# Around the turn between head pairs: where a gate store, a norm read and a staging copy are waited for

## The reference, cut to what matters

```python
h = _rmsnorm(x, W['g_pre_mix'][l])
proj = h @ W['w_in'][l]
qa, fa, ia, ga, qb, kb, vb, uc, gl = jnp.split(proj, _split_points(), axis=-1)
# A) HGRN2: chunkwise gated recurrence, then
oa = _rmsnorm(oa.astype(dt), W['a_norm'][l]) * jax.nn.silu(ga.reshape(Bn, T, A_HEADS, A_DV))
# B) stick-breaking attention over qb, kb, vb; for the samples with K/V from the paged cache
# C) u = ua * sigmoid(ug), causal depthwise conv w=31, LayerNorm, silu
m = gates[:, :, 0] * ya + gates[:, :, 1] * yb + gates[:, :, 2] * yc
out = m @ W['w_o'][l]
```

## Time and profile before

| | us |
|---|---|
| median of 3 runs | 2222.81 (2222.72 to 2224.42) |
| profiled execution, its own time | 2222.81 |
| its span | 2221.0 |
| PE busy in the span | 2048.0 (92%) |
| DVE busy | 1085.8 (49%) |
| ACT busy | 606.7 (27%) |
| POOL busy | 574.7 (26%) |
| DMA, mean rate | 71 GB/s |

### The profile page before, as it was taken

The page is one execution under the profiler, slowest core; times in us unless marked ns, Lnnn a source line. Parts: engine busy times, 40 slices in busy tenths (PEclk is TensorE's granted clock), DMA queues, the critical chain, the costliest instruction groups (busy, mean ns, idle before and its releaser), DMA issues.

```text
span 2221.0 us, 32175 instructions
## 1 busy us (share of the span) xinstructions
PE 2048.0 (92%) x12832; PEld 1957.6 (88%) x12832; DVE 1085.8 (49%) x1169; ACT 606.7 (27%) x792; POOL 574.7 (26%) x392
## 2 busy tenths in 40 slices
PE   6899998999899998999788897799999999999993
PEld 5899997999799997999678897599999999999993
DVE  4187646886387645786247523622221322222136
ACT  3235422462335522562234212310010100101011
POOL 1211211221111211221123323423233332332322
PEclk9999999999899999999899998899999999999997
DMA  4121213111221213112443412111111011111131
GB/s 148 49 88 49 73 45 102 55 60 53 69 89 49 71 39 109 50 61 68 157 150 116 120 60 104 74 33 48 47 38 57 28 52 42 42 54 31 57 111 78
DMA packets 203987, 156.89 MB, mean 71 GB/s; under 512 B 15730, under 2 KB 188402, under 8 KB 203890
## 3 DMA queue, kind: packets, MB, share of 16 engines
q1 hardware_dynamic: 201698, 146.89, 21.3%
q10 hardware_dynamic: 2192, 8.65, 1.0%
HBM read 120.16 MB, written 35.35 MB: 70 GB/s over the span
## 4 chain that ended last, share of the span: by engine, by line
PE 85%; DVE 7%; ACT 4%; DMA 2%; issue 1%; POOL 0%; SPq 0%; POOLq 0%; ACTq 0%; DVEq 0%
PE psum L370 73%; PE psum L674 3%; PE psum L629 2%; PE psum L607 2%; PE psum L618 1%; PE psum L575 1%; DVE hid L1529 1%; PE psum L656 1%; DVE mix L1514 1%; PE psum L638 1%; DMA g_d<-gate_logits 1%; DVE x_again L1508 1%; DVE arena L1206 1%; DMA gates<-g_d 0%; DVE hid_lo L1531 0%
## 5 line engine op out<-in xcount | busy, mean ns | idle before, releaser
L370 PE MATMUL psum<-h_hi,w_hi 128*128 128x352 f32 x2400 | 541.7, 334 | 37.1 <-DVE h_lo L1210 9.9
L370 PE MATMUL psum<-h_lo,w_hi 128*128 128x352 f32 x2400 | 522.0, 326 | 0.0
L370 PE MATMUL psum<-h_hi,w_lo 128*128 128x352 f32 x2400 | 522.0, 325 | 0.0
L370 PEld LDWEIGHTS psum<-h_hi,w_hi 128*128 128x128 f32 x2400 | 407.9, 192 | 63.1 <-issue 41.9
L370 PEld LDWEIGHTS psum<-h_hi,w_lo 128*128 128x128 f32 x2400 | 415.7, 190 | 0.0
L370 PEld LDWEIGHTS psum<-h_lo,w_hi 128*128 128x128 f32 x2400 | 413.6, 191 | 0.0
L360 POOL CAST w_hi<-w_raw 128x512 fp32r<-128x512 f32 (+1 forms) x128 | 97.9, 765 | 733.9 <-PE psum L370 642.7
L347 POOL CAST w_hi<-w_raw 128x1024 fp32r<-128x1024 f32 x60 | 64.1, 1068 | 827.0 <-PE psum L370 807.7
L362 POOL TENSOR_TENSOR w_lo<-w_raw,w_hi 128x512 fp32r<-128x512 f32 (+1 forms) x128 | 227.0, 1773 | 10.3
L1176 ACT ACTIVATE hid<-psum 128x1056 f32<-128x1056 f32 x32 | 33.7, 1054 | 583.1 <-PE psum L370 583.1
L1538 DVE TENSOR_TENSOR ff_sum<-ff_sum,psum 128x1056 f32<-128x1056 f32 x56 | 70.2, 1254 | 227.5 <-PE psum L370 227.5
(11 more groups left out here) (237 smaller groups left out, 2382.3 us busy)
## 6 DMA issues: line engine op xcount, KB each, us to landing
w_raw<-in_w_in SPq DMA_DIRECT2D x60, 512.0 KB, 4.0
w_raw<-in_w_ff SPq DMA_DIRECT2D x32, 512.0 KB, 4.0
w_raw<-in_w_ff SPq DMA_DIRECT2D x64, 256.0 KB, 2.7
g_d<-gate_logits SPq DMA_DIRECT2D x24, 528.0 KB, 2.8
gates<-g_d SPq DMA_DIRECT2D x24, 528.0 KB, 3.7
arena<-in_xT SPq DMA_DIRECT2D x8, 528.0 KB, 7.4
x_again<-in_xT SPq DMA_DIRECT2D x1, 4224.0 KB, 15.2
x_d<-x_again ACTq DMA_DIRECT2D x8, 528.0 KB, 2.7
```

The costliest lines, as they stand in the source:

```text
L370: mm = pe.matmul(ps[:, b0 + g, 0:GW], w[:, slot, k, :], x[:, k, g * GW:(g + 1) * GW], start=(k == 0 and w is wh and x is xh), stop=(k == k ...
```

## The change

Five edits, in the fences below; nothing is computed differently.

1. **Gate stores.** ACT's wait for both gate-store semaphores at the group's end goes. `stage_unit` waits at every gate unit for the last store of its own buffer. The semaphores start at one (`before` = 1, a DVE memset adds it), so that the first group has nothing to wait for.
2. **Norm sums.** H_FILL (4, 4, 4) becomes (4, 4, 2, 2): two of the last four pieces of unit 13 now stand behind the norm sums. ACT copies unit 13 after the two activations of the norm.
3. **The wait for the norm read** moves from the end of PE's group to the start of the next one.
4. **Scores.** In step q = 0 `scores(p, 1, 0)` stands behind the first three pieces, no longer ahead of them.
5. **Turned inputs.** ACT copies unit 8 (and waits for `kv_stored`) after the first level exponential, no longer ahead of the copy of the turned inputs.

```diff
-H_FILL = (4, 4, 4)
+H_FILL = (4, 4, 2, 2)
...
-        n_done, n_read, rs_ready = S("oa_norm_sum", 1), S("oa_norm_read", 1), S("oa_rstd", 1)
+        n_done, n_read, rs_ready = S("oa_norm_sum", 1), S("oa_norm_read", 1, 1), S("oa_rstd", 1)
...
-        gl_stored = [S("gate_stored0", 16 * ((GPG + 1) // 2)), S("gate_stored1", 16 * (GPG // 2))]
+        gl_stored = [S("gate_stored0", 16 * ((GPG + 1) // 2), 1), S("gate_stored1", 16 * (GPG // 2), 1)]
...
                 staged.wait(pe, p, -2)
+                n_read.wait(pe, p, 0)
                 scores(p, 0, 0)
...
-                    if q + 1 < QB:
+                    if q and q + 1 < QB:
                         scores(p, q + 1, 0)
                     fill(A_FILL[0])
+                    if q == 0:
+                        scores(p, 1, 0)
...
                 mm.then_inc(n_done.sem, 1)
-                n_read.wait(pe, p, 1)
+                fill(H_FILL[3])
...
                 if g is not None:
-                    if g >= 2:
-                        gl_stored[g % 2].wait(act, p, 16 * (g // 2))
+                    gl_stored[g % 2].wait(act, p, 16 * (g // 2))
...
                 read_values(QB - 1)
-                if more:
-                    kv_stored.wait(act, p, 32)
-                stage_unit(8, p, more)
                 ia_turned.wait(act, p, 1)
...
                     act.activation(A(B_W[j % 2], n), A(B_D, n), ACT.Exp).then_inc(wexp.sem, 1)
+                    if j == 0:
+                        if more:
+                            kv_stored.wait(act, p, 32)
+                        stage_unit(8, p, more)
...
-                stage_unit(13, p, more)
                 n_done.wait(act, p, 1)
...
                 act.activation(A(B_RS, T), A(B_RS, T), ACT.Exp, scale=-0.5).then_inc(rs_ready.sem, 1)
+                stage_unit(13, p, more)
                 if more:
                     oa_ready.wait(act, p, 1)
                     h_stored.wait(act, p, 32)
-                    for b in range(2):
-                        gl_stored[b].wait(act, p, 16 * ((GPG - b + 1) // 2))
...
+            dve.memset(cwp[:, 1:2], 0.0).then_inc(n_read.sem, 1)
+            dve.memset(cwp[:, 2:3], 0.0).then_inc(gl_stored[0].sem, 1)
+            dve.memset(cwp[:, 3:4], 0.0).then_inc(gl_stored[1].sem, 1)
```

## The result

| | us | ratio to before (95%) |
|---|---|---|
| before | 2222.76 | |
| changed kernel, median | 2197.39 | 0.9872 (0.9851 to 0.9893) |
| changed kernel in a later series of five | 2197.06 | 0.9881 (0.9863 to 0.9899) |

The forecast was 2195.2. One of the four executions of the changed kernel took 6952.75 us, at full clock and for a reason that nothing here shows, and is left out; the other three and the five of the later series lie between 2191.1 and 2198.5. The kernel before spread by 1.9 us in the four executions of the first series and by 9.5 us in the eleven of the later one (2217.8 to 2227.3), so a wider band is not shown. The profiled execution took 2191.1 (span 2189.3), that of the later series 2198.5 (span 2196.7), so I read both.

The account below looks back on a forecast made before the run. PE, busy 92% of the span, bounds the kernel, with cache loads limiting the gain at the turns. First group and turns 22.9, turned inputs 9.2, clock -4.5: 27.6 us off 2222.8 gives 2195.2 us, range 2186 to 2209.

Parts of the forecast that it names:

- The room and the 2.94 us: First group and turns: gain is the cache loads' room, plus 2.94 us per turn from earlier norm sums; 22.9 us.
- The jump is covered but for 1 us: Two turns that jump back: PE's 3.3 us jump runs beside the moved pieces, leaving a 1 us gap.
- ACT's read is no longer waited for: Second scores (L607): PE's waits for ACT's read of the first scores, 19.4 us in four, go.
- The turned inputs give 9.2 us: Ahead of level product 0 (L674): PE's 2.3 us wait for ACT's copy goes in all four groups, 9.2 us.
- the copy of unit 8 is in time: Behind level product 0: ACT's later copy ends before unit 9 needs it, with 0.8 us to spare.
- DVE has some 2.5 us to spare: After the turn: first turned weights are there at about 356 us, and PE wants them at 358.8.
- The clock, -4.5 us: Half clock costs 7.5 us behind new waits at the sample scores; closed gaps at the turned inputs return 3.
- Rival C: Step 1: half clock follows each new wait, costing 40 us against 32; slower, 2231 us; chance 0.04.
- A: Behind level product 0: unit 8's copy comes too late and unit 9 waits; 2207 us; chance 0.12.
- B: Turns: cache loads are not the limit, so the idle goes whole; some 51 us, 2171 us; chance 0.05.
- D: Turn: another link holds ACT, or PE's jump stays uncovered and meets a late clip; within 0.2% of 2222.8; chance 0.03.

Follow-up runs that it names:

- e6: Changed kernel with 16 of each next group's 32 cache loads issued once the products for oa are done, conv_prev directly behind the gate store: 2181.51 us, 0.9813.
- e8: Kernel before with the early cache loads of e6 and none of the five edits: 2222.24 us, 0.9995.
- e4: Changed kernel with the norm sums back behind all four pieces (H_FILL 4, 4, 4, 0): 2203.56 us, 0.9912.
- e2: Kernel before with only the turned-inputs change (unit 8 copied behind the first level exponential): 2207.47 us, 0.9928.
- e7: Changed kernel with the sample scores, and ACT's read of them, moved to the end of step 1: 2192.8 us, 0.9862.
- e10: e7 with three of DVE's conv taps moved from step 0 to steps 2 to 4: 2179.44 us, 0.9809.
- e1: The changed kernel run once more, nothing altered, as a baseline: 2197.06 us, 0.9881.
- e9: Changed kernel with four unused products of ones with kT on PE ahead of the wait for the cache loads: 2193.96 us, 0.9875.
- e3: Changed kernel without the turned-inputs change: 2207.93 us, 0.9933.

## Why the prediction was right, point by point

- *The room and the 2.94 us, not the idle time, are the gain of a turn.* Right, and shown by e6 against e8: the loads set the end in the changed kernel and not in the one before. Waits at L638 of 2.7, 4.5, 4 and 5 us were forecast; they were 2.3, 4.9, 5.0 and 5.7. The three turns gave 18.6 and 17.8 us for 20.2. The term is 1.6 to 2.4 us short. I had `oa_ready` come 2.94 us earlier; it came 2.2 us earlier against the pieces, since DVE's second product took 2.0 us and not 1.3 in each of the three turns, beside POOL's split. That is 2.1 us, and e4, where the split is over, has them back. SP's issue varies beside it: 18.2 to 18.4 us for the 32 loads of a turn where it had been 17.6 to 18.7.
- *The jump is covered but for 1 us.* Right: 0.74 us in the first turn, 0.5 to 1.1 in the profiles of the other runs that have the two pieces there. That it needs the pieces behind the sums as cover was wrong (e4).
- *ACT's read is no longer waited for, in the first group too.* Right.
- *The turned inputs give 9.2 us, and the copy of unit 8 is in time.* Right; e2 shows it by itself. Its gain of 15.9 us is more than the idle and the 3 us of clock that I had put beside it; up to the last norm sums its profile has 9.8 us less idle and 3.7 us less lost to the clock.
- *DVE has some 2.5 us to spare for the first turned weights.* Right for those, but I followed DVE's chain one link too short: its clip of step 1, behind the taps of step 0 and the 2.2 us beside POOL, was nearly as late as the loads. It cost nothing only because the loads covered it (e7, e10).
- *The clock, -4.5 us.* Right in the mean, by luck in part. The term stands for what follows L638: in the table 4.9 + 3.2 and 0.9 + 0.3 us, less the 9.2 of idle, leave -1.1 and -8.0. I had put -7.5 behind the new waits and 3 for the gaps that close at the turned inputs. By half of PE's busy time at half clock, the stretches at L638 cost 5.0 and 5.9 us (the first group's wait of 2.3 us is followed by none), and those at level product 0, 5.0 us, are gone. What I had left out are stretches that follow no gap, in each group behind the sample values (L656), here in the kernel before (the second line is a window with its granted clock, columns as in the earlier trace rows):

```profile
426.95 3.74 PE L656 MATMUL psum<-arena 128*128 128x8 f32 x32
...
430.76:434.18 3.42, 3.42 (x22) 3.09 (x21) 2.97 (x5) 1.88 (x5) 0.00 (x0) 0.50 0.00 0
```

PE is busy all through them and had no gap in the 12 us ahead. They stand in the profiles of both kernels, 17.1 us in all four groups before and after, but 23.9 in that of e1, which has three more of 3.4 us elsewhere where the first profile has one. Rival C puts the slow stretch in work after a turn at 5 us at most, which is misread: in the second turn PE worked at half clock from 605.5 to 611.7, 6.2 us.

**Idle and clock, added up.** PE's idle in the two waits and at the jump went from 39.7 us (19.4 + 9.2, two gaps of 4.8 and one of 1.5) to 19.3, 20.4 less, and the medians gained 25.4 and, in the later series, 26.3. The rest is mostly the clock, and the profiles show it. Up to the last group's norm sums the records of the granted clock have 66.6 us at half clock before, 34.1 in the profile after and 51.2 in the later one; PE was busy for 51.2, 30.4 and 45.7 us of them. How much earlier these sums start is, within 0.7 us in all profiles but that of e9 (which has added work), the sum of two things that went: PE's idle, and half of its busy time at half clock (counted from 60 us on):

| us | sums earlier by | idle | clock |
|---|---|---|---|
| changed kernel | 30.7 | 20.4 | 10.4 |
| e1, the same | 23.1 | 20.1 | 2.8 |
| e2, edit 5 alone | 14.1 | 9.8 | 3.7 |
| e3, all but edit 5 | 18.2 | 11.5 | 7.1 |
| e6, loads early | 41.6 | 31.6 | 10.3 |

The idle of e2 and e3 adds up to that of the whole (21.3 against 20.4 and 20.1). The clock does not (10.8 against 10.4 and 2.8), and so the 5 us by which the parts exceed the whole lie mainly there. The two profiles of the changed kernel differ by 7.4 us in span and by 7.6 in the clock.

Rivals: A falls by e2, B by the waits at L638, C and D by the time. What stays open is why the slow stretches differ from run to run of one program, and why one comes behind the sample values, where PE is busy.

## What to carry to other kernels

Before a wait is removed, look for the next thing that the waiting engine uses and how long it has been there: that room, plus whatever comes earlier on the queue that brings it, is the gain, however long the idle time was. A queue that issues many small transfers one by one is a chain of its own (32 loads, 18 us), and it should be started from the last reader of its buffers, not from the end of the stage. When such a wait is cleared, look one link further on each other engine, since a second one may have been as late under its cover. And when pieces of one engine move, see what the others now do at the same time: here two moved pieces put POOL's split beside DVE's last product and took 0.7 of the 2.94 us back.

## What the runs showed of the hardware

- The jump back of a loop whose body holds some 1600 matmuls took PE's sequencer 3.3 to 3.8 us, against 0.08 us where it falls through. With two pieces (2.94 us) behind the norm sums it began at the sums' end and 0.5 to 1.1 us remained visible; with none, and nothing to wait for, it began 3.8 us ahead of the sums' end and nothing of it was visible (e4).
- DVE's product of 128x1056 took 1.3 us with POOL idle and 2.0 us beside POOL's cast and split; a conv tap of 128x1024 took 1.28 us and 3.48 us beside the split. POOL's split took 3.3 us beside the product and 2.35 alone.
- In a turn in which SP issued the 32 loads of 64 KB in a row, it took 17.6 to 19.0 us from the first to the last, about 0.6 us for each.
- Two profiles of one program differed by 17 us in the time at half clock up to the last norm sums (34.1 and 51.2). Half of PE's busy time in it differs by 7.6 us, about the 7.4 us between their spans.
- Half clock came also without a gap: in each group of every profile a stretch of 3.4 us or more begins under the 32 matmuls of 128x8 (L656 in the kernel before) or within 1.3 us of their end, with PE busy throughout and no gap over 1.1 us in the 12 us ahead of them.
